# Other SBUF base addresses for the moving operands of a two-network kernel

## What is computed

```python
for l in range(DEPTH):
    x = x + 0.5 * swiglu_ffn(rmsnorm(x, ffn1_norm[l]), ffn1_w_up[l], ffn1_w_down[l])
    x = x + mixer(rmsnorm(x, mix_norm[l]), w_in[l], b_in[l], ...)
    x = x + 0.5 * swiglu_ffn(rmsnorm(x, ffn2_norm[l]), ffn2_w_up[l], ffn2_w_down[l])
    x = rmsnorm(x, final_norm[l])
```

```python
for l in range(DEPTH):
    p = rmsnorm_2(x, norm1[l]) @ w_in[l]
    ...
    x = x + mix @ w_o[l]
    up = dwconv_centred(rmsnorm_2(x, norm2[l]) @ w_up[l], conv_w[l], conv_b[l])
    x = x + (jax.nn.silu(gate) * val) @ w_down[l]
```

## Time and profile before

| | us |
|---|---|
| median of 3 runs | 1997.95 |
| lowest and highest run | 1990.9 and 2000.47 |
| the profiled execution: its own time | 2000.59 |
| the profiled execution: its span | 1998.8 |
| PE busy in the span | 1951.2 (98%) |
| DVE busy | 1493.2 (75%) |
| ACT busy | 1078.3 (54%) |
| mean share of the DMA engines, DMA rate | about half, 181 GB/s |

### The profile page before, as it was taken

The page is one execution under the profiler, slowest core; times in us unless marked ns, Lnnn a source line. Parts: engine busy times, 40 slices in busy tenths (PEclk is TensorE's granted clock), DMA queues, the critical chain, the costliest instruction groups (busy, mean ns, idle before and its releaser), DMA issues.

```text
span 1998.8 us, 38956 instructions
## 1 busy us (share of the span) xinstructions
PE 1951.2 (98%) x15906; PEld 1880.4 (94%) x15906; DVE 1493.2 (75%) x2183; ACT 1078.3 (54%) x1358; POOL 31.4 (2%) x40
## 2 busy tenths in 40 slices
PE   6999999999999999999999999999999999999998
PEld 6999998799999999999987999999889999889998
DVE  6555889987755575558899877555788777788777
ACT  5444557566544454445665665444565555566554
POOL 0000011000000000000110000000000000000000
PEclk9999999999999999999999999999999999999999
DMA  6556589534655545555895346555325554335554
GB/s 245 204 183 217 190 243 257 159 101 141 227 200 181 177 146 191 188 201 190 249 258 151 103 141 224 202 181 182 106 106 176 202 182 167 131 124 190 189 191 157
DMA packets 61004, 362.30 MB, mean 181 GB/s; under 512 B 7904, under 2 KB 8160, under 8 KB 24160
## 3 DMA queue, kind: packets, MB, share of 16 engines
q1 hardware_dynamic: 54704, 339.37, 48.9%
q0 software_dynamic: 5184, 18.88, 5.4%
q10 hardware_dynamic: 1008, 2.51, 0.3%
HBM read 353.39 MB, written 1.05 MB: 177 GB/s over the span
## 4 chain that ended last, share of the span: by engine, by line
PE 80%; DVE 14%; ACT 3%; DMA 1%; issue 1%; DVEq 0%; ACTq 0%; SPq 0%
PE bank L439 25%; PE bank L440 24%; PE bank L441 24%; DVE lo L1596 5%; DVE cv L1801 3%; ACT hi L1072 2%; DVE zt L1764 1%; PE bank L655 1%; DMA raw<-in_w 1%; PE bank L628 1%; PE bank L641 1%; DVE n_lo L1600 1%; DMA x<-in_x 1%; DVE qk L1774 1%; DVE sq L1630 0%
## 5 line engine op out<-in xcount | busy, mean ns | idle before, releaser
L1596 DVE TENSOR_TENSOR lo<-raw,hi 128x2048 fp32r<-128x2048 f32 (+1 forms) x336 | 676.4, 2015 | 211.5 <-ACT hi L1072 211.0
L439 PE MATMUL bank<-n_hi,hi 128*128 128x256 f32 x2256 | 638.7, 283 | 25.9 <-DVE lo L1828 12.3
L1072 ACT ACTIVATE hi<-raw 128x2048 fp32r<-128x2048 f32 (+1 forms) x336 | 598.4, 1783 | 113.2 <-PE bank L441 98.2
L440 PE MATMUL bank<-n_lo,hi 128*128 128x256 f32 x2256 | 632.4, 280 | 0.0
L441 PE MATMUL bank<-n_hi,lo 128*128 128x256 f32 x2256 | 632.2, 280 | 0.0
L439 PEld LDWEIGHTS bank<-n_hi,hi 128*128 128x128 f32 x2256 | 429.2, 190 | 32.0 <-DVE lo L1828 12.3
L440 PEld LDWEIGHTS bank<-n_lo,hi 128*128 128x128 f32 x2256 | 426.4, 189 | 1.2 <-issue 1.0
L441 PEld LDWEIGHTS bank<-n_hi,lo 128*128 128x128 f32 x2256 | 426.1, 189 | 0.0
L439 PE MATMUL bank<-h_hi,hi 128*128 128x256 f32 x1152 | 336.0, 292 | 4.4 <-DVE h_lo L1600 3.9
L440 PE MATMUL bank<-h_lo,hi 128*128 128x256 f32 x1152 | 327.4, 284 | 0.0
L441 PE MATMUL bank<-h_hi,lo 128*128 128x256 f32 x1152 | 327.3, 284 | 0.0
(11 more groups left out here) (251 smaller groups left out, 2328.5 us busy)
## 6 DMA issues: line engine op xcount, KB each, us to landing
raw<-in_w SPq DMA_DIRECT2D x286, 1024.0 KB, 4.8
raw<-in_w SPq DMA_DIRECT2D x53, 512.0 KB, 4.0
lo<-in_w POOLq DMA_DIRECT2D x36, 512.0 KB, 9.0
zt<-zt SPq DMA_DIRECT2D x96, 64.0 KB, 5.7
bv<-in_bv SPq DMA_DIRECT2D x2, 768.0 KB, 6.1
spread<-in_spread SPq DMA_DIRECT2D x2, 768.0 KB, 8.0
x<-in_x ACTq DMA_DIRECT2D x4, 256.0 KB, 10.0
out_x<-sq SPq DMA_DIRECT2D x1, 1024.0 KB, 3.9
```

The source lines that it names most:

```text
L439: mm(out, w_hi, a_hi, start=start, stop=False, skip_group_check=True)
L440: mm(out, w_hi, a_lo, start=False, stop=False, skip_group_check=True)
L1072: fn(hi[:, s, 0:w], raw[:, s, 0:w], ACT.Copy).then_inc(sem["hi"], 1)
L1596: v.tensor_tensor(lo[:, s, 0:w], raw[:, s, 0:w], hi[:, s, 0:w].bitcast(F32), ALU.subtract)\
```

## The change

The running counter is moved on by some bytes at three places, and `yt_hi`, `yt_lo` get a place of their own inside their region. No instruction is added, removed or moved: on every engine the same instructions stand in the same order, with other addresses.

```diff
     raw = sb("raw", [P, SLOTS, CW], F32)
     hi = sb("hi", [P, SLOTS, CW], F32R)
     lo = sb("lo", [P, SLOTS, CW], F32R)
+    state["at"] += 448
     x = sb("x", [P, KT, S], F32)
     h_hi = sb("h_hi", [P, KT, S], F32R)
     h_lo = sb("h_lo", [P, KT, S], F32R)
...
+    state["at"] += 416
     at_a = state["at"]
     qk = sb("qk", [P, 24, S], F32)
     s_hi = sb("s_hi", [P, KT, S], F32R, at_a)
     s_lo = sb("s_lo", [P, KT, S], F32R, at_a + KT * S * 4)
+    state["at"] += 192
     at_v = state["at"]
     v_sb = sb("v", [P, 2, GROUPS * 512], F32)
     hid_hi = sb("hid_hi", [P, 2, S], F32R, at_v)
...
-    yt_hi = sb("yt_hi", [P, 4, S], F32R, at_u)
-    yt_lo = sb("yt_lo", [P, 4, S], F32R, at_u + 4096)
+    yt_hi = sb("yt_hi", [P, 4, S], F32R, at_u + 384)
+    yt_lo = sb("yt_lo", [P, 4, S], F32R, at_u + 4480)
```

## The result

The changed kernel takes 2009.9 us (median of 5 runs, 2009.13 to 2014.88). The kernel before, with two more runs than it had ahead of the prediction, takes 1997.95 us (median of 5, 1989.58 to 2003.66). The ratio is 1.0067, with a 95% interval of 1.0042 to 1.0093. The forecast was 1970 us and faster; the time lies inside its range, on the wrong side of no change. The profiled execution is 2009.39 us, against 2000.59 before.

What follows compares the result with a forecast made beforehand. PE was taken as the bound: the number of `mm3` matmuls times the distance between their starts. Gains of 12.3 (`h`) and 16.4 us (`n`, `hid`) sum to 28.7, giving about 1970 us, range 1944 to 2025.

Steps and rivals of the forecast that it cites:

- Rival 2: Distance to the weights isn't what decides the pace; 1998 us, or 1991 to 2004 by luck of the blocks; chance 0.15.
- Step `h`, 0 to 448: `mm3` matmuls of `h` leave 120.0 ns; gain between 0 and 18.8 us, taken as 12.3, a half of each pace.
- its sign in the load times: In the stretch of `h` at 228 to 284 us, the weight loads were to read 188 ns.
- Step `n` and `hid`, 192 to 224: Feed-forward `mm3` matmuls take both paces in equal parts; gain 16.4 us, bounds 32.8 gain to 22.9 loss.
- The lost fast block: Last feed-forward block, 1238 matmuls at 113.3 ns; going to 120.0 would lose 8.3 us, counted in the loss bound only.
- Step `s` and `yt`: Mixer projections, 192 to 32 and 96; could only lose, 3.8 us at most, taken as nothing.
- Steps `last` and `end`, DVE, ACT, DMAs: `last` and `end`, 128 to 160, gain at most 2.6 us; other engines and DMAs on moved tensors cost nothing; all taken as nothing.
- The convolution tap: DVE row L1801, reading `upad`; was to stay at its median of 477 ns.
- Rival 3: Odd multiples of 32 put `n`, `hid`, `s`, `yt` at `h`'s slow pace; 2019 to 2025 us; chance 0.30.
- Its mark, loads of 192 ns on all lines: Sign of Rival 3: weight loads of `n` read 192 ns on all lines.

Runs made afterwards that it cites:

- e15: Kernel before plus 56 PE-only streams behind its last product, in the order of `pairs`, seven starts at each of eight distances; 2671.58 us, one run.
- e2: Kernel before with only `n` and `hid` moved, 192 to 224 from the weights; 2013.64 us, ratio 1.0088.
- e10: Changed kernel plus six small matmuls of 8 columns, one ahead of each feed-forward loop; 2008.54 us, one run.
- e13: Kernel before plus 52 PE-only streams of 90 matmuls behind its last product, at set distances, some with own and next weights apart; 2596.66 us.
- e1: Kernel before with only `h` moved, 0 to 448 from the weights; 1985.98 us, ratio 0.9963.
- e3: Kernel before with everything, weights included, moved up 32 bytes, all distances kept; 1993.49 us, ratio 0.9994.
- e4: Kernel before with `h` at 64, `s` at 320, `yt` at 224, `last` at 192, `n` and `hid` kept at 192; 1972.32 us, one run.
- e5: Kernel before with all moving operands at 192 from the weights; 1988.74 us, ratio 0.9971.
- e7: Kernel before plus a small matmul of 8 columns at the start of each feed-forward turn, 52 in all; 1983.01 us, one run.
- e9: Kernel before plus one small matmul of 8 columns ahead of each feed-forward loop, six in all; 1983.48 us, ratio 0.9939.
- e12: As e11, with the table `const` that the small matmuls read moved back from distance 192 to 0; 1983.72 us, ratio 0.9929 to the kernel before.
- e11: As e5, plus small matmuls ahead of each feed-forward loop and at most mixer chunks; 1981.82 us, ratio 0.9930 to the kernel before.
- e14: Kernel before with `h` at 448 and a small matmul at the start of each feed-forward turn, 52 in all; 1978.58 us, ratio 0.9918.
- e8: Kernel before with `lo`, `n_lo` and `hid_lo` 32 bytes further than their high parts, and `h` at 192; 2015.85 us, one run.

## Why the prediction was wrong

**The view of the problem was right.** The time is the count of `mm3` matmuls times the distance between their starts. Each distance to the weights has shown its own short list of paces, and at 192 there are two, 113.3 and 117.8 ns. Rival 2 falls: e15 has equal matmuls at 113.3 to 120.0 ns with only distance and start changed: 113.3 or 117.8 at 192, 116.7 at 32, 120.0 at 0. What the streams lose at the slower distances, no run shows.

**Step `h`, 0 to 448: right.** The gain taken was 12.3 us, half of each of two paces. It measured 9.5. The stretch runs at 117.7 ns, other chunks of `h` at 113.4. Only its sign in the load times was off: a load of 192 ns is still there on one line.

**Step `n` and `hid`, 192 to 224: the one that failed.** It gave a gain of 16.4 us, on the ground that "both paces" of 192 would be found at 224 as well, in equal parts. It measured a loss of 13.5. At 224 the runs showed a single pace, 118.3, next to the slow one of 192 (117.8), and no fast one. The step took the nearest row, 32 bytes away, for the place itself. e2, e10 and e15 show it: alone, in the whole, and with nothing beside. The bounds held, +32.8 to -22.9. The text had even said why the middle was a guess: no row had an odd multiple of 32. A gain was at stake that only a fast pace could bring, and the share of the fast pace was set at a half without a row that bore on it. That a shift of the streams against each other redraws the pace was an estimate of the author; the runs show both paces with `n` and `hid` left at 192 (21 fast blocks of 42, below), and 118.3 alone at 224. With three distances in the trace, of which one had a fast pace, one in three was the better guess for a new one. Then the likeliest case is `h`'s 12.3 us less the 6 to 8 us of the last block's fast pace: some 5 us faster, which is no measurable change.

**The lost fast block** was in the bounds of that step (8.3 us for 1238 matmuls), but not in its middle. In what was measured it is the largest part of the loss: that block went from 113.3 to 118.3 ns, 1238 x 5 = 6.2 of 13.5 us. Then come 0.55 ns for each matmul of the other blocks, 7063 x 0.55 = 3.9 us. The 3.4 us left lie outside these stretches, where short stretches of `n` had been fast too.

**The one fast block of six was a poor draw, and the step took it for the kernel's state.** e13 and e15 run the kernel before unchanged up to its last product. In e13 its third block reads

```profile
723.00:897.00 174.00, 174.00 (x1533) 173.94 (x1532) 108.31 (x106) 79.90 (x81) 0.00 (x0) 1.00 0.57 199
```

where the earlier trace rows has 1478 matmuls in the same 174 us. Three of its six blocks are fast in e13, two in e15, one in the profile that the prediction read. With e1, e3, e4 and e5, where `n` and `hid` stand at 192 as well, it is 21 of 42. Equal parts is thus what 192 already gives, at each execution and without any change of address. If 224 had had both paces in equal parts, as the step assumed, the median would have moved by about nothing and not by 16.4 us (an estimate from these counts). It also fits that the ratio of the runs, 0.67% or 13 us, shows more loss than the two profiled executions, 8.8 us.

**Step `s` and `yt`: mis-sized.** Taken as nothing, with 3.8 us as the most. It measured 2.5: `s` at 32 takes 116.7 ns, `yt` at 96 takes 120.0. Their 113.3 before was a draw as well: at the same 192 they ran at 117.8 in e1.

**Steps `last` and `end`, DVE, ACT, DMAs: right.** They were taken as nothing. `last` and `end` gained 0.8 us, and DVE and ACT are busy 1.3 and 2.9 us longer. The other matmuls, which the prediction doesn't name, lost 3.0 us with their waits; what did that wasn't told apart. The convolution tap:

```profile
L1804 DVE SCALAR_TENSOR_TENSOR cv<-upad,prm,cv x480: 386/481/509, 247.5 to 1130.7; 128x256 f32<-128x256 f32 x160
```

Its median is 481 ns where the earlier trace rows has 477: 480 x 4 ns = 2 us of DVE's work. Whether any of it reaches the end wasn't told apart.

**Rival 3** was nearest in its sign, wrong in its reason and its size. Odd multiples of 32 as such did nothing (e3, ratio 0.9994), 32 has 116.7 and 160 can have 117.3, both better than `h`'s old 120.0. Its mark, loads of 192 ns on all lines, isn't there: they read 188 on all three, at 118.3 ns a matmul. The load time is no sign of the pace here: 188 ns goes with 113.3 and with 118.3.

**The forecast's spread.** The five runs of before lie 14 us apart, those of the changed kernel 6, those of e2 4. With `n` at 192 one to five of the six blocks were fast in the seven profiles counted above; at 224 (the changed kernel, e2, e10) all six ran at 118.3 ns in each of three.

## What to carry to other kernels

Where PE is the bound and all its matmuls are equal, count the matmuls of several stretches before you take a pace as given. Two values for the same code, here 113.3 and 117.8 ns, mean that there may be something to win. The distance in SBUF between the moving and the stationary operand, modulo 256 bytes, was worth 113.3 to 120.0 ns a matmul here, so treat it as a parameter of the kernel like a tile size: measure a short stream at each of eight distances behind the kernel's own work (one run, 56 streams, 670 us) and read the whole list, rather than forecast one distance from its neighbour. Compare the list's best and worst draw, and time the result over ten or more runs, since a good distance with two paces gives a median and not a value (e5, all at 192: 1978 to 1999 us in 12 runs). For the same reason one profile of such a kernel isn't its state: take two or three. Two distances were left untried in a kernel's large groups: 32, which gave 116.7 and nothing else in all 11 streams, and 112, which gave 113.3 in its only one.

## What the runs showed of the hardware

- The pace of fp32r matmuls (128x128 weights, 256 columns) with a weight load each went by the distance modulo 256 bytes of their operands in SBUF: 113.3 to 120.0 ns at multiples of 32, the same with PE alone as in the kernels (e13, e15), and 123.3 at 4 bytes (e13, one stream), where 0 has 120.0. That distance and distance + 256 are alike was tried at multiples of 32 (16 pairs, within 0.03 ns).
- The paces repeat closely. At 64 in e15 the four fast streams have means of 113.33 to 113.35 ns and the three slow ones of 117.78 to 117.80, with none between. Why a distance has these paces and no others, no run shows: no view names what the two streams share.
- The pace was seen to change where the stream was broken: at a small matmul of 8 columns (e7 and e9, 117.8 to 113.3; e12, 113.3 to 117.8) and after waits that put two starts 0.28 and 0.55 us apart (e9, 113.3 to 117.8). One program drew one, three and two fast blocks in three executions (before, e13, e15). Which start leads to which pace stays open. In e7 and e9 the small matmul led to the fast one each time, in e11 and e12 it went both ways, and in e14 two blocks stayed slow past it.
- With `n` and `hid` kept at 192 from the weights that load beside them and moved from their own by 32 in two matmuls of three, the pace was 118.9 or 119.1 ns (e8). In e13 the distance to the next weights, moved alone, changed the pace in six of six streams (120.0 at 0 to 118.9 and 118.3), that to the own weights in four of six (120.0 to 118.6 with 32): both count. How the two combine wasn't found.
